# Scores from stacked rounded parts that pass through DRAM, one key block in round 0, and the sample attention in another order

## The chip, the cores and the metric

One core of one Trainium2 chip. The metric is the device time of one execution in microseconds (us), as the median of a few runs.

## The reference

One layer of a decoder for a prompt of 1024 tokens and 8 samples of 4 tokens (1056 tokens, `TOK`), all in float32, with 16 query heads of 64 on 4 key heads, a window of 128, and a mixture of 32 experts behind it. What matters here is the attention:

```python
q, k, v, xl, yl, ga, gr = split(h @ w_in)          # h = norm(x) * (1 + scale) + shift
q, k = rope(q), rope(k)
s = einsum('...qhgd,...khd->...hgqk', q, k) * 64 ** -0.5
s = where(0 <= q_pos - k_pos <= 128 and k_pos >= 0, s, -1e30)
m = maximum(max(s), sink);  p = exp(s - m)
o = (p / (sum(p) + exp(sink - m))) @ v
```

For the prompt it is banded: a block of 128 queries sees its own 128 keys and the 128 before. The first block has nothing before it. A sample sees 128 cached keys and its 4 new ones. A recurrent branch (convolution, gates, scan, GeLU) runs on `xl` and `yl`; both branches, the output projection and the experts follow.

## The kernel before

Every engine has a list of instructions written out by hand, and they meet in semaphores. A float32 product is either an f32 matmul or three products of rounded parts: `up` is the value rounded to the engine's fp32r format, `low` what is missing, and up x up + up x low + low x up comes close to the exact product (`three`, `project`). Values lie with features on the partitions; the 1056 tokens are three groups of 352 columns (`GC`), here called thirds.

1. **Projections of k, v and q** (60 to 197 us). Per chunk of 128 features, `project` makes three thirds of 24 products; ScalarE takes them out of PSUM (`keep`), copies them with halves exchanged (`swap`), and VectorE rotates (`rope`) into `kT` and `oT`. `m` counts the chunks from 2 to 9 for the queries. In between TensorE computes pieces of the adaLN vector from `w_ada` (`ada_piece`, tiles `wlate`, two buffers; SP loads piece n once piece n - 2 is used). SP's queue also holds the next weights (`wA`, `wB`) and the stores of the rounded activations (`h_store`).
2. **Sample attention** (198 to 233 us): `first_out(0)` (the first third of the next projection), pieces 14 and 15, the scores of all 8 samples in one go, `first_out(1)`, softmax on VectorE and ScalarE, transposes, 64 small products with the cached values, `first_out(2)`.
3. **Eight rounds** (233 to 580 us), one for each block of 128 queries. A round has 8 units; a unit has two heads of 64 features on the two halves of the partitions. GpSimd copies each half of `oT` into `qst`, whose other half is zero (L961), and one f32 matmul a head with all 128 partitions of `kT` gives 128 x 256 scores (previous and own block; round 0 has a zero block before). VectorE masks and takes the maximum (`first`, L1613), ScalarE exponentiates (L1186), VectorE scales (`second`, L1623 and L1624), TensorE transposes a unit later (L2320), VectorE or ScalarE copies (L1704, L1212), TensorE multiplies with the values, ScalarE puts the outputs in place of the queries in `oT` (L1215), from where SP stores them. Between a round's units stand 12 projection and gate products of the recurrent branch (`outs`, spread by `halves_at`), and VectorE and ScalarE do the convolution, gates and scan of the chunk before (`conv`, `lru_step`). Round 0 has the other adaLN products instead (`slab`, 16 loads of 0.5 MB by `slab_half` into a ring of four).

In `pe_round` a unit's place is this, s counting from 0 to 9:

```python
scores(s);  slab(s) if begin else outs(i, s);  transposes(s - 1);  values(s - 2)
```

so the transposes of unit 4 stand behind the scores and projection products of unit 5. The order of the engines' lists around it is fixed. Behind the rounds follow the projections of both branches, the router and the experts, which the change leaves alone.

Of the kernel before, what the change touches and what calls it, by code (L numbers as in the profile page):

```python
# [17 lines left out]
P = 128  # L18
D = 1024
# [159 lines left out]
def build(nc, I, O):  # L179
    ctx = ExitStack()  # L180
    with ctx:
# [11 lines left out]
        oT = at("oT", [P, KC, TOK], big)  # L193
# [61 lines left out]
        masks = at("masks", [P, BLKS, 2 * P], wv0, BF16)  # L255
# [21 lines left out]
        pS = at("pS", [P, NB, P + NT], tmp0 + 512)  # L277
        pZ = at("pZ", [P, NB * 36], tmp0 + 512 + 1056)
        pTs = at("pTs", [P, NB, P], tmp0 + 512 + 1056 + 288)
        pTn = at("pTn", [NS, NB, P], tmp0 + 512 + 1056 + 288 + 1024)  # L280
        ss0 = tmp0 + 512 + 1056 + 288 + 2048
# [6 lines left out]
        qst = at("qst", [P, 4, 2, P], u0)  # L288
        pp = at("pp", [P, 2, 2, 2 * P + 1], u0 + 1024)
        pT = at("pT", [P, 2, 4, P], u0 + 1024 + 1024 + 32)  # L290
# [153 lines left out]
        hp_dram = [nc.dram_tensor(n, [P, KC, TOK], F32) for n in ("hp_up_dram", "hp_low_dram")]  # L444
        o_dram = nc.dram_tensor("o_dram", [P, KC, TOK], F32)
# [8 lines left out]
        ld_c, ld_first, ld_small, ld_late = sem("ld_c"), sem("ld_first"), sem("ld_small"), sem("ld_late")  # L454
        ld_wada = [sem(f"ld_wada{i}") for i in range(PIECES)]
        ld_rows = [sem(f"ld_rows{i}") for i in range(LF)]
        ld_rope, ld_kc, ld_wV = sem("ld_rope"), sem("ld_kc"), sem("ld_wV")
# [3 lines left out]
        ld_spread, ld_samples, ld_route, ld_xin, ld_masks = sem("ld_spread"), sem("ld_samples"), sem("ld_route"), sem("ld_xin"), sem("ld_masks")  # L461
# [12 lines left out]
        pads_set = sem("pads_set")  # L474

# [6 lines left out]
        u_staged, u_scores, u_negmax, u_exp = sem("u_staged"), sem("u_scores"), sem("u_negmax"), sem("u_exp")  # L482
# [33 lines left out]
        st_side, st_kws = sem("st_side"), sem("st_kws")  # L516
# [14 lines left out]
        def lane_part(ap, lane):  # L531

            return ap[NS * lane:NS * (lane + 1), 0:FD].rearrange("r (h c) -> r h c", h=2)

# [67 lines left out]
        def _(sp):  # L602

            sp.dma_start(cT[:, :, :], I["cT"]).then_inc(ld_c, 16)
# [35 lines left out]
            sp.dma_start(cosT[:, :], I["cos"]).then_inc(ld_rope, 16)  # L640
            sp.dma_start(sinT[:, :], I["sin"]).then_inc(ld_rope, 16)
# [4 lines left out]
            for n in range(4, 10):  # L646
                ada_piece(n)
                if n in (5, 6):
                    sp.dma_start(kcx[:, n - 5, :, 0:P], I["kcT"][:, n - 5]).then_inc(ld_kc, 16)
                if n == 7:  # L650
                    sp.dma_start(vc[:, :, :], I["v_cache"].rearrange("b k n -> k b n")).then_inc(ld_kc, 16)
            for m in range(2, 10):
# [7 lines left out]
                if m == 9:  # L660
                    for n in (14, 15):
                        ada_piece(n)
                h_store(m - 2)
# [18 lines left out]
            def o_store(i):  # L682

                sp.wait_ge(u_out, 4 + KC * (i + 1))
                sp.wait_ge(st_o, 16 * (i + 1))
                sp.dma_start(o_dram[:, :, i * P:(i + 1) * P], oT[:, :, i * P:(i + 1) * P]).then_inc(st_o, 16)
# [35 lines left out]

            slab_half(16)
            slab_half(17)
            sp.wait_ge(s_pe, 1)
            sp.wait_ge(st_kws, 32)
            slab_half(18)
            sp.wait_ge(s_pe, 6)
            slab_half(19)
            sp.wait_ge(s_dve, 9)  # L730
            sp.dma_start(o_dram[:, :, SEQ:TOK], oT[:, :, SEQ:TOK]).then_inc(st_o, 16)
# [4 lines left out]
            for i in range(1, KC):  # L736
                lg_weights(i)
                o_store(i - 1)
# [5 lines left out]
            sp.wait_ge(u_out, 4 + KC * BLKS)  # L744
# [183 lines left out]
            sp.wait_ge(st_side, 16 * 4)  # L928
            sp.wait_ge(st_kws, 32)

        @block.gpsimd
        def _(pool):
# [7 lines left out]

            pool.wait_ge(h_split, KC)
            pool.wait_ge(hs_stage, 3 * PIECES)
            pool.memset(kT[:, :, 0:P], 0.0).then_inc(pads_set, 1)
            pool.memset(vtok[:, 0, :], 0.0).then_inc(pads_set, 1)

            pool.wait_ge(rope_done, 10)
            pool.wait_ge(v_kept, TILES)
            pool.wait_ge(s_dve, 9)
            pool.wait_ge(st_kws, 32)
            pool.wait_ge(ld_small, 16 * N_SMALL)  # L950
            pool.wait_ge(ld_late, 16 * N_LATE)
            pool.wait_ge(ld_masks, 16)
            pool.memset(qst[:, :, :, :], 0.0).then_inc(u_staged, 1)
            pool.wait_ge(u_staged, 1)
            pool.sem_inc(u_out, 4)
            for i in range(BLKS):
                for u in range(KC):
                    pool.wait_ge(u_out, 8 * i + u + 1)
# [60 lines left out]
        def _(act):  # L1019
# [7 lines left out]
            act.wait_ge(ld_c, 16)  # L1027
# [43 lines left out]
            act.wait_ge(pads_set, 2)  # L1071
# [23 lines left out]
            for t in range(TILES):  # L1095
# [3 lines left out]
                if t == 4:  # L1099
                    round_pair(0, 2)  # L1100
            act.wait_ge(v_kept, TILES)

            act.dma_start(masks[:, :, :], I["masks"]).then_inc(ld_masks, 16)
# [4 lines left out]
            act.dma_start(O["kwp"], kT[:, :, SEQ:SEQ + P]).then_inc(st_side, 16)  # L1108
            for m in range(2, 10):
# [1679 lines left out]
```

## Time and profile before

| | |
|---|---|
| median of 3 runs | 1685.8 us (1685.08 to 1690.02) |
| the profiled execution | 1685.88 us, its span 1684.0 us |
| TensorE (PE), its weight loads (PEld) | 95%, 69% of the span |
| VectorE (DVE), ScalarE (ACT), GpSimd (POOL) | 44%, 37%, 8% |
| mean granted TensorE clock | 0.983 of full speed |
| DMA | 404.66 MB, mean 240 GB/s |
| copy with rounding, 128 x 1024, ScalarE | 1.06 us |
| difference of rounded parts, 128 x 1024, VectorE | 1.23 us |
| maximum with mask of 256 columns, and scaling of 256, spacing on VectorE | 0.40 us, 0.27 us |
| copy of 512 columns out of PSUM, VectorE | 0.60 us |

How to read it: TensorE's share is that of a span in which its instructions overlap, so a high share says that it seldom waits, not that it is at its peak. The granted clock is 1.00 at 2.4 GHz and 0.50 at 1.2 GHz; a value between is a mean over a stretch with both. PE MATMUL rows of f32 products count two instructions for one matmul.

### The profile page before, as it was taken

The page shows a single profiled execution, that of the slowest core. Times are in us where ns is not written, and L with a number is a line of the kernel's source. Part 1 is how long each engine was busy: PE and PEld are TensorE (multiplying, and loading weights), DVE is VectorE, ACT ScalarE, POOL GpSimd, SP SyncE. Part 2 cuts the span into 40 slices and gives each one's busy share as a digit, 9 for nine tenths or more (in the row PEclk, how much of TensorE's full clock was granted, in tenths as well). Part 3 has the DMA queues.
Part 4 walks back from the last instruction along what each step waited for, and adds up shares of the span by engine and source line. Part 5 has one row for each costly group of instructions (what it writes and reads, how often), then busy time and mean ns, then how long its engine had stood idle before and what let it go on. Part 6 is the DMA issues. An engine that isn't in the chain of part 4 may idle for free. (4 is left out here: it accounts for less than half of the span.)

```text
span 1684.0 us, 27184 instructions
## 1 busy us (share of the span) xinstructions
PE 1601.7 (95%) x11089; PEld 1161.9 (69%) x11089; DVE 743.4 (44%) x1468; ACT 625.8 (37%) x1130; POOL 126.9 (8%) x218
## 2 busy tenths in 40 slices
PE   6999989999999989999999999988998999999997
PEld 2889877888888889999999989762333333333344
DVE  3523446888888773454555457670000000000006
ACT  4526435666666653343444354411110111111113
POOL 0000011111111000000000030000000000000012
PEclk9999999999999999999999999988999999999998
DMA  9464561111111286373457564879999999999988
GB/s 359 169 212 154 163 209 60 54 46 51 54 54 55 73 290 202 125 275 126 135 174 234 188 203 147 338 280 391 424 398 428 425 425 423 406 408 399 408 326 318
DMA packets 98866, 404.66 MB, mean 240 GB/s; under 512 B 13431, under 2 KB 42135, under 8 KB 85800
## 3 DMA queue, kind: packets, MB, share of 16 engines
q1 hardware_dynamic: 86736, 380.23, 59.6%
q0 software_dynamic: 6992, 17.78, 2.7%
q10 hardware_dynamic: 5016, 4.93, 1.0%
q8 instruction: 88, 1.44, 0.4%
q14 instruction: 34, 0.28, 0.1%
HBM read 364.83 MB, written 44.32 MB: 243 GB/s over the span
## 5 line engine op out<-in xcount | busy, mean ns | idle before, releaser
L1236 ACT ACTIVATE wup<-wraw 128x1024 fp32r<-128x1024 f32 x120 | 126.7, 1059 | 266.0 <-PE ps L2109 221.5
L1730 DVE TENSOR_TENSOR wlow<-wraw,wup 128x1024 fp32r<-128x1024 f32 x112 | 136.9, 1224 | 148.9 <-ACT wup L1236 148.3
L2109 PE MATMUL ps<-wg,xT 128*32 128x512 f32 (+2 forms) x1072 | 156.8, 612 | 11.4 <-DMA wg<-w_gate 10.6
L2109 PE MATMUL ps<-wd,aT 128*32 128x512 f32 (+2 forms) x1072 | 148.5, 593 | 6.8 <-DMA wd<-w_down 5.4
L2109 PE MATMUL ps<-wu,xT 128*32 128x512 f32 (+2 forms) x1072 | 150.3, 597 | 3.3 <-DMA wu<-w_up 3.3
L2109 PE MATMUL ps<-h_up,wup 128*128 128x384 f32 (+1 forms) x384 | 125.7, 327 | 3.5 <-DVE wlow L1730 3.5
L2109 PE MATMUL ps<-h_up,wlow 128*128 128x384 f32 (+1 forms) x384 | 124.5, 324 | 0.0
L2109 PE MATMUL ps<-h_low,wup 128*128 128x384 f32 (+1 forms) x384 | 124.5, 324 | 0.0
L2109 PEld LDWEIGHTS ps<-wd,aT 128*32 128x32 f32 (+2 forms) x1072 | 46.8, 117 | 105.1 <-issue 103.3
L2109 PEld LDWEIGHTS ps<-wg,xT 128*32 128x32 f32 (+2 forms) x1072 | 44.9, 119 | 105.7 <-issue 102.5
L1186 ACT ACTIVATE pp<-pp,ngm 128x257 f32<-128x257 f32 x128 | 64.3, 504 | 122.8 <-DVE ngm L1613 122.2
L2109 PEld LDWEIGHTS ps<-wu,xT 128*32 128x32 f32 (+2 forms) x1072 | 46.4, 117 | 91.8 <-issue 89.8
L2109 PE MATMUL ps<-hp_up,wA_up 128*128 128x352 f32 x312 | 108.5, 348 | 1.1 <-DVE hp_low L1490 1.1
L2109 PE MATMUL ps<-hp_up,wB_up 128*128 128x352 f32 x312 | 106.1, 340 | 1.6 <-ACT gB L1162 1.6
L2109 PE MATMUL ps<-hp_low,wA_up 128*128 128x352 f32 x312 | 102.0, 327 | 0.0
L2109 PE MATMUL ps<-hp_up,wA_low 128*128 128x352 f32 x312 | 101.9, 327 | 0.0
L2109 PE MATMUL ps<-hp_up,wB_low 128*128 128x352 f32 x312 | 100.7, 323 | 0.0
L2109 PE MATMUL ps<-hp_low,wB_up 128*128 128x352 f32 x312 | 100.6, 323 | 0.0
L1426 ACT ACTIVATE aT<-ps 128x512 f32<-128x512 f32 x20 | 11.9, 597 | 230.1 <-PE ps L2602 230.1
L2051 DVE TENSOR_TENSOR sgm<-sgm,ps 128x512 f32<-128x512 f32 x20 | 13.8, 688 | 167.7 <-ACT sgm L1418 167.7
L961 POOL COPY qst<-oT 64x128 f32<-64x128 f32 x128 | 57.1, 446 | 278.9 <-ACT oT L1215 274.5
L2109 PEld LDWEIGHTS ps<-h_up,wup 128*128 128x128 f32 x384 | 73.1, 190 | 4.7 <-issue 4.4
(416 smaller groups left out, 3243.6 us busy)
## 6 DMA issues: line engine op xcount, KB each, us to landing
wg<-w_gate SPq DMA_DIRECT2D x32, 2048.0 KB, 14.8
wu<-w_up SPq DMA_DIRECT2D x32, 2048.0 KB, 15.4
wd<-w_down SPq DMA_DIRECT2D x32, 2048.0 KB, 14.1
wraw<-w_ga SPq DMA_DIRECT2D x24, 512.0 KB, 3.5
wraw<-w_gr SPq DMA_DIRECT2D x24, 512.0 KB, 3.9
wraw<-w_at SPq DMA_DIRECT2D x24, 512.0 KB, 3.5
wraw<-w_lr SPq DMA_DIRECT2D x24, 512.0 KB, 3.5
wraw<-w_out SPq DMA_DIRECT2D x24, 512.0 KB, 3.7
```

What stands on the lines that cost most here:

```text
L961: pool.tensor_copy(qst[half, u % 4, a, :], oT[half, u, i * P:(i + 1) * P]).then_inc(u_staged, 1)
L1186: ins = act.activation(pp[:, s % 2, a, :], pp[:, s % 2, a, :], ACT.Exp, bias=ngm[:, s % 2, a:a + 1], scale=-1.0, accum_out=sme[:, s % 2, a ...
L1236: act.activation(wup[n % UP][:, :, :], wraw[n % RAW][:, :, :], ACT.Copy).then_inc(w_rounded, 1)
L1426: act.activation(aT[:, :, :], ps[:, 6, :].rearrange("p (m c) -> p m c", c=P), ACT.Copy).then_inc(a_kept, 1)
L1730: V.tensor_tensor(low_part(n)[:, :, :], wraw[n % RAW][:, :, :], wup[n % UP][:, :, :].bitcast(F32), ALU.subtract).then_inc(w_split, 1)
L2051: V.tensor_tensor(sgm[:, :], sgm[:, :], ps[:, 2, :], ALU.mult).then_inc(ch_moe, 1)
L2109: return pe.matmul(out, lhsT, rhs, start=start, stop=stop, skip_group_check=True)
```

## The change

It has five parts.

- **Parts of q and k.** ScalarE rounds the 1024 prompt columns of each key chunk and each rotated query chunk, VectorE subtracts, SP stores both parts to `k_dram` and `q_dram`: eight stores of 64 partitions x 2 x 1024 for the keys (each half head twice), four of 64 x 1024 for each query chunk.
- **Scores.** For a head, `qst` holds the upper part of its 64 features on partitions 0 to 63 and the lower part on 64 to 127; `kst` holds the keys' upper part twice over each other, and their lower part likewise. Two rounded products, accumulated, take the place of one f32 product. SP loads keys by block (two buffers) and queries by half block (three); GpSimd's copies and its two memsets go.
- **Round 0** works on the own block alone: 128 columns in scores, mask, exp, scaling, transposes, copies, values. One mask remains.
- **Sample attention** in the order below, softmax by bank and by half.
- **Outputs** go to `oS` and `oSs`, which wait for the store of the round before.

```diff
+            sp.wait_ge(kq_split, 2)
+            for part in range(2):
+                for a in range(2):
+                    for half in range(2):
+                        sp.dma_start(head_rows(k_dram, half).rearrange("d (p a) x n -> d p a x n", p=2)[:, :, a, part, :],
+                                     head_rows(k_part(part), a)).then_inc(st_kq, 16)
+            def q_store(u):
+                sp.wait_ge(kq_split, u + 3)
+                sp.wait_ge(st_kq, kq_stored(u))
+                for part in range(2):
+                    for a in range(2):
+                        sp.dma_start(head_rows(q_dram, part)[:, u, a, :], head_rows(q_part(u, part), a)).then_inc(st_kq, 16)
...
+            def load_keys(i):
+                if i < BLKS:
+                    ge(sp, u_scores, KC * (i - 1))
+                    c0 = P if i == 0 else 0
+                    sp.dma_start(kst[i % 2][:, :, :, c0:2 * P].bitcast(F32),
+                                 k_dram[:, :, :, (i - 1) * P + c0:(i + 1) * P]).then_inc(ld_kq[i % 2], 16)
+            def load_queries(n):
+                if n < 2 * BLKS:
+                    i, u0 = n // 2, 4 * (n % 2)
+                    ge(sp, u_scores, 4 * (n - 3) + 4)
...
+                    sp.dma_start(qst[n % 3][:, :, :, :].bitcast(F32), q_dram[:, u0:u0 + 4, :, i * P:(i + 1) * P]).then_inc(ld_kq[i % 2], 16)
...
+            sp.wait_ge(st_kq, kq_stored(KC))
+            sp.wait_ge(s_dve, 6)
+            load_keys(0)
+            load_queries(0)
+            load_queries(1)
...
+            load_keys(1)
+            load_queries(2)
...
+                load_queries(2 * i + 1)
+                load_keys(i + 1)
+                load_queries(2 * i + 2)
                 o_store(i - 1)
...
-                    for a in range(2):
-                        half = slice(HD * a, HD * a + HD)
-                        pool.tensor_copy(qst[half, u % 4, a, :], oT[half, u, i * P:(i + 1) * P]).then_inc(u_staged, 1)
...
+                        if s == 2:
+                            act.wait_ge(st_o, 16 * (i + 1))
+                            act.wait_ge(st_kq, kq_stored(KC))
+                        act.activation(oS[:, s - 2, :], ps[:, 7, 0:P], ACT.Copy).then_inc(u_out, 1)
...
-            first_out(0)
-            ada_piece(14)
-            ada_piece(15)
+            for o in range(2):
+                first_out(o).then_inc(proj_done, 1)
...
-            first_out(1)
-            pe.wait_ge(s_dve, 8)
+            ada_piece(14)
+            ada_piece(15)
+            first_out(2, range(0, 2))
...
-                            out = ps[:, 3 + s % 2, a * 2 * P:(a + 1) * 2 * P]
-                            ins = mm(out, qst[:, s % 4, a, :], kT[:, s // 4, bass.ds(i * P, 2 * P)], True, True)
+                            out = ps[:, 3 + s % 2, a * 2 * P + c0:(a + 1) * 2 * P]
+                            for part in range(2):
+                                ins = mm(out, qst[n % 3][:, s % 4, a, :], kst[i % 2][:, 2 * (s // 4) + a, part, c0:], part == 0, part == 1)
```

How the change moves instructions, at two places. First TensorE, the sample attention before: from the end of `first_out(0)` (the last `hp_up,wA_low` above) the pieces of w_ada (`wlate`), mask and scores of the samples (`mask_s`, `kcx`), and later, behind 24 products of `first_out(1)`, the transposes (`ident`) and the values (`vtok`, `vc`).

```order
L2109 MATMUL ps<-wlate_96,cE 32x512 x2
L2109 MATMUL ps<-wlate_97,cE 32x512 x2
L2109 MATMUL ps<-mask_s,identb 128x132
L2109 MATMUL ps<-kcx,qs 32x132 x4
...
L2265 MATMUL ps<-ident,pS 128x128 x4
L2269 MATMUL ps<-ident,pZ 32x128 x4
L2265 MATMUL ps<-ident,pS 128x128 x4
L2269 MATMUL ps<-ident,pZ 32x128 x4
L2109 MATMUL ps<-pTn,vtok 64x128 x4
L2109 MATMUL ps<-pTs,vc 64x16 x32
L2109 MATMUL ps<-hp_up,wA_up_98 128x352
```

The same engine now, from the sample scores, which follow `first_out(1)`, to the end of the values; of the projection products one of each piece of `first_out(2)` stands.

```order
L2194 MATMUL ps<-mask_s,identb 128x132
L2194 MATMUL ps<-kcx,qs 32x132 x4
L2194 MATMUL ps<-wlate_104,cE 32x512 x2
L2194 MATMUL ps<-wlate_105,cE 32x512 x2
...
L2353 MATMUL ps<-ident,pS 128x128 x4
L2357 MATMUL ps<-ident,pZ 32x128 x4
L2353 MATMUL ps<-ident,pS 128x128 x4
L2357 MATMUL ps<-ident,pZ 32x128 x4
L2194 MATMUL ps<-hp_up,wA_up_106 128x352
...
L2194 MATMUL ps<-pTn,vtok 64x128 x4
L2194 MATMUL ps<-pTs,vc 64x16 x32
L2194 MATMUL ps<-hp_up,wA_up_106 128x352
```

The pieces have moved behind the scores, and the last third is cut into three: 6 products ahead of the transposes, 6 behind them, 12 behind the values. Second, SP's queue at the end of the key projections, before: pieces 8 and 9 of w_ada, then 10 and 11, then the weights of the next chunk and the first store of activations.

```order
L625 DMA wlate_96<-w_ada 128x1024
L625 DMA wlate_97<-w_ada 128x1024
L625 DMA wlate_96<-w_ada 128x1024
L625 DMA wlate_97<-w_ada 128x1024
L659 DMA wA<-w_qk 128x1024
L634 DMA hp_up_dram<-hp_up 128x1056
```

And now:

```order
L646 DMA wlate_104<-w_ada 128x1024
L646 DMA wlate_105<-w_ada 128x1024
L677 DMA k_dram<-oT 128x1x1024 x8
L646 DMA wlate_104<-w_ada 128x1024
L646 DMA wlate_105<-w_ada 128x1024
L695 DMA wA<-w_qk 128x1024
L655 DMA hp_up_dram<-hp_up 128x1056
```

Eight stores of the keys' parts stand between piece 9 and piece 10.

## Rows read from the trace of the kernel before

**Rows 1.** The page: busy time, share of the span and instructions of each engine.

```profile
PE 1601.7 (95%) x11089; PEld 1161.9 (69%) x11089; DVE 743.4 (44%) x1468; ACT 625.8 (37%) x1130; POOL 126.9 (8%) x218
```

**Rows 2.** Busy time by stage: stretch, its length, engines' busy us, clock, DMA share, GB/s.

```profile
100.00:195.00 95.00, 95.00 (x578) 89.70 (x578) 35.70 (x29) 49.41 (x59) 0.00 (x0) 1.00 0.50 166
220.00:232.00 12.00, 11.20 (x103) 10.63 (x102) 0.55 (x3) 2.02 (x4) 3.25 (x9) 0.72 0.65 184
410.00:455.00 45.00, 44.55 (x292) 39.17 (x291) 37.01 (x97) 28.33 (x69) 7.73 (x16) 1.00 0.16 51
```

**Rows 3.** TensorE in order of time, round 4, then value projection: start, us, engine, instruction.

```profile
404.35 1.03 PE L2109 MATMUL ps<-kT,qst 128*128 128x256 f32 x4
...
405.38 0.32 PE L2109 MATMUL ps<-hp_low,wA_up 128*128 128x352 f32 x1
...
76.58 0.28 PE L2109 MATMUL ps<-wV_up,hp_up 128*128 128x256 f32 x1
76.70 0.29 PE L2109 MATMUL ps<-wV_low,hp_up 128*128 128x256 f32 x1
```

**Rows 4.** VectorE, ScalarE and TensorE in order of time, round 4.

```profile
406.01 0.26 DVE L1611 COPY pp<-nsink 128x2 f32<-128x2 f32 x1
419.32 0.17 DVE L1611 COPY pp<-nsink 128x2 f32<-128x2 f32 x1 [1.21 <-PE ps L2109]
423.25 2.28 DVE L1665 TENSOR_TENSOR_SCAN olst<-gC,xc 128x1024 f32<-128x1024 f32 x1
428.96 0.35 DVE L1624 TENSOR_SCALAR pp<-pp,rcp 128x256 f32<-128x256 f32 x1
...
419.41 1.28 ACT L1186 ACT_TABLE_LOAD   x1
...
429.37 0.66 PE L2320 MATMUL ps<-ident,pp 128*128 128x128 f32 x4
441.30 0.60 PE L2320 MATMUL ps<-ident,pp 128*128 128x128 f32 x4
```

**Rows 5.** Waits from 275 to 575 us: who for whom, us in total, times, longest.

```profile
PEld ps L2320 <- DVE pp L1624: 3.4, 7, 0.8
```

**Rows 6.** End of round 0: TensorE and VectorE in order of time, then stretches.

```profile
263.44 1.11 PE L2320 MATMUL ps<-ident,pp 128*128 128x128 f32 x4 [3.30 <-DVE pp L1624]
...
271.67 1.03 PE L2109 MATMUL ps<-kT,qst 128*128 128x256 f32 x4
...
248.50 0.16 DVE L1611 COPY pp<-nsink 128x2 f32<-128x2 f32 x1
263.03 0.35 DVE L1624 TENSOR_SCALAR pp<-pp,rcp 128x256 f32<-128x256 f32 x1
...
265.00:275.00 10.00, 10.00 (x45) 6.90 (x42) 1.49 (x8) 5.16 (x13) 1.14 (x4) 0.80 0.19 59
```

**Rows 7.** TensorE in order of time, sample attention.

```profile
205.67 1.05 PE L2109 MATMUL ps<-wlate,cE 128*32 128x512 f32 x4 [3.26 <-DMA wlate<-w_ada]
...
219.42 0.66 PE L2265 MATMUL ps<-ident,pS 128*128 128x128 f32 x4 [3.20 <-DVE pZ L1589]
...
222.19 0.65 PE L2109 MATMUL ps<-pTn,vtok 32*64 32x128 f32 x8 [0.80 <-ACT pTn L1131]
222.78 4.37 PE L2109 MATMUL ps<-pTs,vc 128*64 128x16 f32 x64
...
232.99 1.02 PE L2109 MATMUL ps<-kT,qst 128*128 128x256 f32 x4
```

**Rows 8.** DMA issues: transfer, queue, count, KB each, median us to landing.

```profile
wslab<-w_ada SPq DMA_DIRECT2D x16, 512.0 KB, 4.8
```

**Rows 9.** SP's issues, TensorE's use of piece 10, and one us of stores.

```profile
104.06 0.33 SPq L625 DMA_DIRECT2D wlate<-w_ada  x1
...
118.05 1.05 PE L2109 MATMUL ps<-wlate,cE 128*32 128x512 f32 x4
...
144.00:145.00 1.00, 1.00 (x9) 1.00 (x8) 0.29 (x1) 0.97 (x2) 0.00 (x0) 1.00 1.01 414
```

More of the change, by code:

```diff
@@ L192, in build @@
         hT = at("hT", [P, KC, TOK], 0)
[L193 removed]
+        oT, q_low = at("oT", [P, KC, TOK], big), at("q_low", [P, KC, TOK], big, F32R)
+        kst = [at(f"kst{i}", [P, 4, 2, 2 * P], w, F32R) for i, w in enumerate((big, big + 5 * D))]
+        qst = [at(f"qst{i}", [P, 4, 2, P], big + (2 + i) * D, F32R) for i in range(3)]
+        oS, oSs = at("oS", [P, KC, P], big + 7 * D), at("oSs", [P, KC, NS], big + 8 * D)
         hp_low, hp_up = at("hp_low", [P, KC, TOK], 0, F32R), at("hp_up", [P, KC, TOK], 2 * big, F32R)
@@ L533, in lane_part, with k_part, q_part, kq_stored @@
             return ap[NS * lane:NS * (lane + 1), 0:FD].rearrange("r (h c) -> r h c", h=2)
+        def k_part(part):
+            return oT[:, 2 + 2 * part:4 + 2 * part, 0:SEQ]
+        def q_part(u, part):
+            return q_low[:, u, 0:SEQ].bitcast(F32) if part else oT[:, (u + 3) % KC, 0:SEQ]
+        def kq_stored(units):
+            return 16 * 8 + 64 * units
+        def head_rows(ap, a):
+            return ap[HD * a:HD * a + HD]
         def bc(ap, shape):
@@ L1181, in act_round @@
             def act_round(i, first=False):
+                c0 = P if first else 0
                 for s in range(KC + 2):
@@ L1563, in _, with split_query @@
                     split_pair(0, 2)
+            for p in range(2):
+                dve.wait_ge(kq_rounded, p + 1)
+                V.tensor_tensor(k_part(1)[:, p].bitcast(F32R), kT[:, p, P:P + SEQ], k_part(0)[:, p], ALU.subtract).then_inc(kq_split, 1)
+            def split_query(u):
+                dve.wait_ge(kq_rounded, u + 3)
+                V.tensor_tensor(q_low[:, u, 0:SEQ], oT[:, u, 0:SEQ], q_part(u, 0), ALU.subtract).then_inc(kq_split, 1)
             for m in range(2, 10):
                 split_pair((m + 1) % 2, (m + 1) // 2 + 1)
+                if m > 2:
+                    split_query(m - 3)
                 rope(m, oT[:, m - 2, :])
@@ L2270, in _ @@
                 ins.then_inc(s_pe, 1)
+            first_out(2, range(2, 4))
             pe.wait_ge(s_act, 5)
@@ L2317, in pe_round @@
                         for a in range(2):
-                            for hf in range(2):
+                            for hf in blocks:
                                 q = 2 * a + hf
@@ L2730, in constants @@
     out = np.float32(-1e30)
-    masks = np.zeros((P, BLKS, 2 * P), np.float32)
-    masks[:, :, :P] = np.where(k >= q, 0, out)[:, None, :]
-    masks[:, :, P:] = np.where(k <= q, 0, out)[:, None, :]
-    masks[:, 0, :P] = out
+    masks = np.zeros((P, 2 * P), np.float32)
+    masks[:, :P] = np.where(k >= q, 0, out)
+    masks[:, P:] = np.where(k <= q, 0, out)
     t, j = (m % NT)[:, None], np.arange(P + NT)[None, :]
```

226 lines of the change are left out of this document (126 added, 100 removed).

## The prediction

> **What bounds the kernel now.** I read the page first, then the busy time by stage, then the order in time of single stretches, then the waits. TensorE is busy for 95% of the span [rows 1], so the question in every stage is whether it is the engine that the stage ends on. In the projection stage (100 to 195 us) it never pauses and the DMA engines are half used; in the 12 us before the attention rounds its clock is at 0.72 on average; a later round keeps it 44.5 of 45 us busy, but VectorE is busy for 37.0 of 45 beside it [rows 2]. The orders in time show its waits, in the sample attention and in round 0. So there are three places to cost, and everything behind 580 us moves with them.
>
> **Later rounds (1 to 7).** One unit's two f32 score products take 0.87 us: first at 404.35, and the second projection product starts at 405.38, of which 0.16 is its own spacing [rows 3]. The new form is four rounded products with the same 256 columns. Rounded products with 256 columns start 0.12 us apart in the value projection [rows 3], so 0.48: 0.39 saved a unit, 3.1 a round, if TensorE sets the pace. It doesn't quite. In round 4 VectorE takes up unit 0 at 406.01 and from there its work is a chain: it pauses once for TensorE (1.21 us before 419.32), but the exp of unit 3 cannot start before 420.7 anyway, because ScalarE has a table load (419.41, 1.28 us) ahead of it, behind the square root. Then come the scan (2.28 us) and unit 4, whose scaling is at 428.96, and TensorE's transposes of unit 4 start at 429.37, when that is done [rows 4]. TensorE waits there already: 7 times from 275 to 575 us, 3.4 us in all on the weight side [rows 5]. From 406.01 to 429.3 are 23.3 us that lose nothing. From 429.37 to 441.30 (11.9 us) TensorE sets the pace and saves two score units, 0.78. From there the chain is evacuation, square, gate products, tanh, two VectorE passes, until VectorE takes the next unit 0; it holds no scores, so it stays. The third part is what is left of the period, (404.35 - 271.67) / 3 = 44.2 us [rows 3, 6]: 9.0. I take 0.78 + 0.06 for the wait gone = 0.84 a round, 5.9 in seven. Bounds: 0.3 a round (only the present wait goes) to 3.1. GpSimd's 16 copies a round (L961) go, and nobody waits for them: nothing. Late next is VectorE. In their place SP issues 2 MB of loads a round; the DMA engines are 0.16 busy there [rows 2], and the loads are for a later half round or the next round, so they hide. They stand ahead of the store of the outputs, whose landing ScalarE now awaits before unit 0 of the next round is written. It writes that just before the table load at 419.4, 15 us after the round's first scores [rows 3, 4]; 2.6 MB at 319 GB/s (51 / 0.16) take 8 us, and with 2 or 3 for issue and landing some 4 are left. If that cover goes, each us is paid in each round, since ScalarE's table load is behind it.
>
> **Sample attention.** Now TensorE waits 3.26 us for piece 14 of w_ada until 205.67, has the sample scores behind pieces 14 and 15, waits 3.20 for the softmax before 219.42 and 0.80 before 222.19, runs much of the 64 small products (4.37 us) and of the last projection third at half clock, and begins round 0 at 232.99 [rows 2, 7]. In the new order the second projection third (24 products 0.16 apart, 3.85 us) is ahead of the scores and the two pieces behind them. Step by step, with the durations of now: thirds 0 and 1 until 206.0; scores 4.2 (as now, from 207.9 to 212.1), until 210.1; VectorE's three maxima go along by bank and end at 211.2; the last exps and the sum until 212.5; half the scaling 213.7, the other half 215.3 (an addition of 0.69 is between them); transposes until 216.3, copies 217.0; 0.6 for eight products and 64 x 0.05 (half of which ran so before the clock fell) until 221; the last half of third 2, 1.92, until 222.9. The last query part must be rounded (1.06), split (1.23), stored and, with block 0 of the keys, loaded again before the first scores; SP awaits all stores for that. Its 1 MB follows about 4.7 MB that are queued from 197.4 on. With the store rate below it is back at 223.5. **9.5 us earlier** (bounds 8 and 10).
>
> **Round 0.** It lasts 38.7 us (232.99 to 271.67), with VectorE the bound at its end: TensorE waits 3.30 us for it before 263.44, and then has a clock of 0.80 [rows 6]. One key block halves the softmax work. By the rows, max 0.40 to about 0.27 and scaling 0.27 to about 0.15, twice a unit, the copy 0.60 to 0.35 for every other: VectorE's units 4 to 7 last 12.3 us instead of 14.9 (248.50 to 263.4). But the adaLN slabs don't get shorter. They pass a ring of four, 4.8 us to landing [rows 8]; with the products on them a unit takes 2.75 us at best, and ahead of slabs 20 and 21 there now are 1.5 MB more (keys of block 1, queries). I place slab 2 at 10.5 us into the round (now 6.5), unit 4 at 14.5, and 12.3 + 6.5 for the chain and the gates: 33.3. **5.4 us less** (bounds 3.5 and 9). The 128-column rounded products have no row; four of them cost between 0.24 (half of 0.48) and 0.87, and neither end decides, since slabs and VectorE do.
>
> **What is added before.** Ten roundings on ScalarE (1.06) and ten subtractions on VectorE (1.23) lie in stages where these are 49 and 36 of 95 us busy: nothing. The stores are another matter. Eight stores of 0.52 MB, 4.2 MB in all, go into SP's queue behind piece 9 (issued at 104.06) and ahead of piece 10, which TensorE uses at 118.05 [rows 9]. Each takes 64 partitions; no row shows such a store. Bounds: the rate of full-width stores, 414 GB/s [rows 9], 10 us; or the same bytes per partition and second, 207, 20 us. The nearest row is the full-width store in the same queue, but the second reading breaks no row either, and opposite halves follow each other and may overlap: I take the middle, 15 us. From 107 (piece 9 is through) to 122, piece 10 at 124.5: a wait of 6.5 (bounds 1.5 and 12). Such a gap may drop the clock: now 3.2 us of waiting are followed by about 7 us at half speed, which cost 0.28 of 12 us, 3.4 [rows 2, 7]; I take 1.5 (bounds 0 and 3.4). **8 us more** (1.5 to 15). Later iterations (three thirds, 11.5 us) hold 2.6 MB, and hide at either rate.
>
> The Trainium skill (SBUF — State Buffer, "Door 1: The DMA port swizzle") says that 64 partitions reach 8 of 16 ports, and that a 1 MiB transfer on them moves 196 GB/s against 328 on all; under "Can I just issue two DMAs to hit both halves?" it says they serialize. It speaks against my middle value; by it, called an estimate, the stores last 21 us and piece 10 is 13 us late. No row here shows it.
>
> **Sum**: +8 - 9.5 - 5.4 - 5.9 = -12.8 us. The profiled execution is at 1685.88 us (its span 1684.0), the median of the runs at 1685.8, so both give 1673.
>
> **Rivals.**
> 1. *Half-rate stores.* For it: the layout, half the partitions in each store. Against: alternate halves can overlap. Wait and clock +15, round 0 only 8 earlier and 3.5 shorter, rounds -5.9: -2.4, so 1683. This is the case in which the rule quoted above holds.
> 2. *Full-rate stores.* +1.5, -10, -7, -5.9: 1664.
> 3. *TensorE keeps the pace in the rounds.* If VectorE's chain gives way (GpSimd leaves it more of the memory, or the exp moves up), 3.1 x 7 = 22 instead of 5.9: 1657. Against it: the wait at every unit 4.
> 4. *Slower than before.* One mechanism, the key stores ahead of piece 10 in SP's queue. From about 180 GB/s downwards (23 us) they eat all gains; at 150 they last 28 us, piece 10 waits 20, with 3.4 for the clock; round 0 then is 5 earlier and 3 shorter: 23.4 - 5 - 3 - 5.9 = +9.5, so 1695. For it: the output copies of ScalarE's queue run at the same time. Against: stores of 4 KB runs reach 414 now.
> 5. *It doesn't do what it says*: rounded products with two operands of their own as dear as the f32 ones. Then the rounds give 0.3 or less, the rest stays: 1678. The value projection's rows speak against it; it lies inside the forecast's range.
>
> **How the numbers follow.** A measurement of this kernel tells some 0.3%, 5 us, from no change: 1680.7 to 1690.9 is "the same". Forecast with rival 5: 0.35 (its own range 1665 to 1681); rival 1: 0.27; rival 2: 0.13; rival 3: 0.12; rival 4: 0.13. Faster: 0.34 + 0.13 + 0.12 and 0.08 of rival 1 = 0.67; same: 0.01 + 0.19 = 0.20; slower 0.13. The range from 1657 to 1690 leaves out half of rival 3 and most of rival 4.
>
> **What would show it.** TensorE's wait for wlate near 118 us: 6.5 us right, under 2 rival 2, over 11 rival 1, 20 rival 4. Sample scores right behind the second third, and no half clock before round 0. First scores near 223.5 plus the wait's delay. In round 0 waits for wslab rather than for VectorE. Rounds 43.2 us apart, with about 2 us of TensorE idle before the unit 4 transposes; 41 us apart would be rival 3, over 44 a wait for the output store. I'd be wrong if the wait for stored parts before round 0 is over 5 us, or if a later stage changes its length.

## The result, and the profile after

The median went from 1688.5 us (9 runs) to 1696.3 us (9 runs): ratio 1.0046, 95% interval 1.0025 to 1.0067, so slower by 0.5%. The forecast was 1673, the range 1657 to 1690. The profiled execution of the changed kernel has a span of 1691.7 us against 1684.0.

The page of the changed kernel (busy us of each engine, share of the span, instructions):

```profile
PE 1578.2 (93%) x11041; PEld 1145.4 (68%) x11041; DVE 748.9 (44%) x1484; ACT 635.4 (38%) x1140; POOL 68.5 (4%) x87
```

Stretches of it: start and end, length, busy us of each engine, granted clock, share of the DMA engines, GB/s.

```profile
100.00:195.00 95.00, 84.79 (x501) 78.60 (x500) 37.93 (x31) 48.33 (x57) 0.00 (x0) 0.95 0.71 241
107.00:124.00 17.00, 9.31 (x54) 7.79 (x52) 3.77 (x3) 5.27 (x6) 0.00 (x0) 0.90 0.96 283
237.58:280.31 42.73, 30.76 (x605) 23.07 (x605) 21.44 (x84) 17.01 (x63) 0.00 (x0) 0.73 0.69 238
322.02:365.22 43.20, 40.50 (x287) 35.94 (x285) 35.58 (x97) 27.41 (x68) 0.00 (x0) 1.00 0.33 101
365.22:409.93 44.71, 42.00 (x286) 37.12 (x285) 35.67 (x97) 27.76 (x68) 0.00 (x0) 0.96 0.32 99
409.93:456.04 46.11, 43.40 (x287) 38.53 (x285) 35.68 (x97) 27.77 (x68) 0.00 (x0) 0.93 0.31 95
```

TensorE does 23.5 us less work, and the span is 7.7 us longer: it now waits. Between 100 and 195 us it is busy for 84.8 us where it never paused [rows 2], round 0 (237.58 to 280.31) has a clock of 0.73 with the DMA engines 0.69 busy, and rounds 2, 3 and 4 (the last three) do the same work in 43.2, 44.7 and 46.1 us. The waits of TensorE (who for whom, us in total, times, longest):

```profile
PE ps L2414 <- DVE pp L1707: 15.8, 8, 2.4
...
PE ps L2194 <- DMA wslab<-w_ada: 11.2, 6, 6.5
PE ps L2194 <- DMA wlate<-w_ada: 11.1, 2, 10.2
...
PE ps L2194 <- DMA qst<-q_dram: 5.0, 1, 5.0
```

Before the change VectorE's `pp` stood there with 4.0 us, `wlate` with 3.9 and `wslab` with 0.8, and `qst` had no wait. In these four the two traces differ most. Cut at the same instructions in both traces, the stages are (us):

| stage | before | after | difference | forecast |
|---|---|---|---|---|
| start to piece 6 of w_ada | 95.2 | 93.4 | -1.8 | 0 |
| piece 6 to piece 12 (projections) | 102.1 | 114.4 | +12.3 | +8 |
| piece 12 to the first scores | 35.7 | 29.8 | -5.9 | -9.5 |
| round 0 | 38.7 | 42.7 | +4.1 | -5.4 |
| rounds 1 to 7, until the wait for `gB` | 310.8 | 312.0 | +1.2 | -5.9 |
| from there to the end | 1101.6 | 1099.4 | -2.2 | 0 |
| sum | 1684.0 | 1691.7 | +7.7 | -12.8 |

The first and the last row are not the change's: over the profiles of all kernels here but g, the last stage lies between 1096.7 and 1101.6 and the start between 93.2 and 98.1, in no order that follows the edits. Round 0 spreads as well: up to its end the changed kernel, b and c (below) have the same code, and it lasts 42.7, 44.2 and 47.4 us in their traces, at clocks of 0.73, 0.69 and 0.62. So +4.1 is the low end of what these traces show there. Behind the other four stand these rows, in order of time (start, us, engine, line, instruction, count, [idle before <- what ended it]): TensorE at piece 10, SP's key stores, TensorE ahead of round 0 and at slab 2, and SP in the same stretch.

```profile
126.51 1.92 PE L2194 MATMUL ps<-wlate,cE 128*32 128x512 f32 x4 [10.21 <-DMA wlate<-w_ada]
...
102.61 15.38 SPq L677 DMA_DIRECT2D k_dram<-oT  x8
...
237.58 1.08 PE L2194 MATMUL ps<-kst,qst 128*128 128x128 f32 x4 [5.02 <-DMA qst<-q_dram]
...
253.76 2.27 PE L2194 MATMUL ps<-wslab,cE 128*32 128x64 f32 x64 [6.51 <-DMA wslab<-w_ada]
...
220.53 3.68 SPq L686 DMA_DIRECT2D q_dram<-oT  x2
...
226.04 1.57 SPq L651 DMA_DIRECT2D wslab<-w_ada  x2
...
230.19 0.60 SPq L731 DMA_DIRECT2D kst<-k_dram  x1
230.83 7.00 SPq L741 DMA_DIRECT2D qst<-q_dram  x2
237.94 0.99 SPq L651 DMA_DIRECT2D wslab<-w_ada  x2
...
239.59 0.86 SPq L731 DMA_DIRECT2D kst<-k_dram  x1
240.50 4.16 SPq L741 DMA_DIRECT2D qst<-q_dram  x1
...
245.35 14.48 SPq L651 DMA_DIRECT2D wslab<-w_ada  x8
```

TensorE waited 10.2 us for piece 10, which SP could issue only after 15.4 us of key stores. Ahead of round 0 it waited 5.0 us for the stored queries. In round 0, slab 2 came 16.2 us after the first scores (253.76 - 237.58), where it came at 6.5 before: SP spent 7.0 us on the two loads of queries, since the second waits for the landing of the first, and had the halves of slab 1 and everything behind it still to issue. TensorE in order of time, round 4 (before it, the unit 4 transposes of round 2):

```profile
347.20 0.65 PE L2414 MATMUL ps<-ident,pp 128*128 128x128 f32 x4 [2.39 <-DVE pp L1707]
...
430.06 0.74 PE L2194 MATMUL ps<-kst,qst 128*128 128x256 f32 x4
...
435.12 1.12 PE L2414 MATMUL ps<-ident,pp 128*128 128x128 f32 x4 [2.40 <-DVE pp L1707]
...
437.22 1.23 PE L2194 MATMUL ps<-kst,qst 128*128 128x256 f32 x4
```

One of the units behind the first three in round 4 before the change, and that round as a stretch:

```profile
436.49 1.13 PE L2109 MATMUL ps<-kT,qst 128*128 128x256 f32 x4
...
404.35:448.43 44.08, 43.63 (x285) 38.25 (x284) 36.09 (x97) 27.50 (x67) 7.72 (x17) 1.00 0.16 52
```

The four score products take 0.58 us of TensorE at full clock (0.74 less the 0.16 by which the next product overlaps), where two f32 ones took 0.97 (1.13 less 0.16). That is 0.39 a unit, as forecast, and TensorE's busy time in a round falls by 3.1 us, from 43.63 to 40.50 (round 2 above). But the wait for unit 4 is 2.40 us long now, and behind it the transposes last 1.12 instead of 0.65 and the four score products 1.23 instead of 0.74: the clock is at its half level, 1.2 GHz. In round 2 the wait is as long (347.20) and the clock stayed full.

### The profile page after: what moved, and what is told of

The parts are those of the page before. It is cut to its first block and busy times, and to the rows that moved or that the text cites. A ratio compares the mean times of both kernels' runs of the same rounds, so it can differ in the third digit from the quotient of the medians.

```text
span 1691.7 us, 27036 instructions
## 1 busy us (share of the span) xinstructions
PE 1578.2 (93%) x11041; PEld 1145.4 (68%) x11041; DVE 748.9 (44%) x1484; ACT 635.4 (38%) x1140; POOL 68.5 (4%) x87
## 5 line engine op out<-in xcount | busy, mean ns | idle before, releaser
L2194 PEld LDWEIGHTS ps<-wd,aT 128*32 128x32 f32 (+2 forms) x1072 | 47.0, 117 | 106.0 <-issue 104.2
L2194 PEld LDWEIGHTS ps<-wg,xT 128*32 128x32 f32 (+2 forms) x1072 | 44.7, 119 | 106.0 <-issue 102.8
L1246 ACT ACTIVATE pp<-pp,ngm 128x257 f32<-128x257 f32 (+1 forms) x128 | 62.6, 491 | 116.7 <-DVE ngm L1696 116.0
L2194 PE MATMUL ps<-hp_up,wA_up 128*128 128x352 f32 x312 | 101.7, 326 | 1.3 <-DVE hp_low L1554 1.3
L2131 DVE COPY xT<-ps 128x512 f32<-128x512 f32 x21 | 14.5, 692 | 134.1 <-PE ps L2661 134.0
## 6 DMA issues: line engine op xcount, KB each, us to landing
wu<-w_up SPq DMA_DIRECT2D x32, 2048.0 KB, 15.4
```

Of the source, the lines that this page charges most:

```text
L1246: ins = act.activation(pp[:, s % 2, a, c0:], pp[:, s % 2, a, c0:], ACT.Exp, bias=ngm[:, s % 2, a:a + 1], scale=-1.0, accum_out=sme[:, s % ...
L2131: V.tensor_copy(xT2[n % 2][:, 4:8, :], ps[:, 1, :].rearrange("p (k c) -> p k c", c=P)).then_inc(x_high_half, 1)
L2194: return pe.matmul(out, lhsT, rhs, start=start, stop=stop, skip_group_check=True)
```

## The experiments

All ratios are to the kernel before the change, measured in the same session, from 7 to 10 runs of each kernel, but only four of e, g, j, k and l; the changed kernel's is 1.0046. The stages come from one trace of each. The stages are those of the table above, in us: projections / to first scores / round 0 / rounds 1 to 7.

| kernel | ratio (interval) | projections | to scores | round 0 | rounds 1-7 |
|---|---|---|---|---|---|
| before | 1 | 102.1 | 35.7 | 38.7 | 310.8 |
| after | 1.0046 (1.0025-1.0067) | 114.4 | 29.8 | 42.7 | 312.0 |
| a_keys_behind | 1.0060 (1.0039-1.0082) | 117.6 | 31.1 | 47.7 | 313.3 |
| b_fill | 1.0011 (0.9992-1.0030) | 115.4 | 29.8 | 44.2 | 304.1 |
| c_half_moved | 0.9952 (0.9932-0.9973) | 114.6 | 30.0 | 47.4 | 294.1 |
| d_slabs_first | 1.0031 (1.0018-1.0045) | 115.3 | 32.5 | 39.3 | 313.3 |
| e_full | 0.9865 (0.9826-0.9904) | 103.5 | 30.6 | 38.7 | 294.4 |
| f_before_moved | 0.9991 (0.9971-1.0012) | 102.1 | 39.4 | 39.3 | 307.8 |
| g_full_width | not used, see there | 109.9 | 33.0 | 44.0 | 311.9 |
| h_spread | 1.0017 (0.9993-1.0040) | 103.7 | 32.0 | 43.9 | 313.4 |
| i_one_block | 0.9961 (0.9942-0.9980) | 102.1 | 35.4 | 35.7 | 310.7 |
| j_pieces_first | 0.9815 (0.9796-0.9834) | 104.1 | 27.8 | 36.9 | 294.5 |
| k_before_best | 0.9933 (0.9916-0.9950) | 102.1 | 39.1 | 35.6 | 307.8 |
| l_busy_wait | 0.9875 (0.9856-0.9894) | 106.0 | 31.2 | 39.4 | 294.5 |

**Rounds: is it the clock?** b repeats the scores of unit 5, useless work in front of the wait:

```diff
-                        for a in range(2):
+                        for a in (0, 1) if begin or s != 5 else (0, 1) * 6:
                             out = ps[:, 3 + s % 2, a * 2 * P + c0:(a + 1) * 2 * P]
```

> The changed kernel; in rounds 1 to 7 TensorE repeats the four score products of unit 5 five more times (20 useless products, about 2.4 us), just ahead of the place where it waits 2.4 us for unit 4. Theory (the clock falls behind that wait and costs 1.5 us a round in rounds 3 to 7): more work, and the rounds last 43.2 us each at a full clock, 8 us less in all: 1688. Rival (the longer rounds come from VectorE or from the loads): the rounds stay at 44.7 or grow, and the time is 1696 or more.

Round 4 of b as a stretch:

```profile
414.21:457.39 43.18, 42.87 (x306) 38.35 (x305) 35.55 (x97) 27.39 (x68) 0.00 (x0) 1.00 0.32 102
```

Rounds 2 to 6 last 43.2 us each at full clock, with 20 products more in them, and rounds 1 to 7 last 304.1 us instead of 312.0. That is 7.9 us by the trace and 0.35% (6 us) between the ratios, whose intervals overlap a little, so the trace tells it more firmly than the times. The clock theory held.

c and f put useful work there, the first half of output 4, in the changed kernel and in the one before:

```diff
-            return (((0, 0),), ((0, 1), (1, 0)), ((1, 1), (2, 0)), ((2, 1),), ((3, 0),), ((3, 1),), ((4, 0), (4, 1)), ((5, 0), (5, 1)),
+            return (((0, 0),), ((0, 1), (1, 0)), ((1, 1), (2, 0)), ((2, 1),), ((3, 0),), ((3, 1), (4, 0)), ((4, 1),), ((5, 0), (5, 1)),
```

> The changed kernel; in the rounds the first half of output 4 (12 products, 2.0 us) stands in unit 5's place, ahead of the wait for unit 4, instead of in unit 6's. Theory (TensorE has 2 us of free time there and sets the pace behind it): no wait over 0.5 us, no half clock, and rounds of about 41.5 us instead of 44.6 on average: 20 us less, 1676. Rival (VectorE's chain sets the round's end too): the rounds stay at 43.2, 9 us less, 1687. If neither the wait nor the clock matters: 1696.

> The kernel before the change, with only the half of output 4 moved ahead of the wait for unit 4. Theory (there TensorE waits only 0.5 us for unit 4, and only the 2 us of that half are moved, not saved): rounds shorter by 0.3 to 0.5 us, 3 us in all, 1686. Rival (the move alone is worth what it was worth in the changed kernel): 16 us, 1673; then the rounded scores would have no part in that gain.

TensorE in round 4 of c, in order of time:

```profile
436.53 0.66 PE L2414 MATMUL ps<-ident,pp 128*128 128x128 f32 x4 [0.45 <-DVE pp L1707]
...
448.04 0.66 PE L2414 MATMUL ps<-ident,pp 128*128 128x128 f32 x4 [1.10 <-DVE pp L1707]
```

That round as a stretch:

```profile
411.37:453.41 42.04, 40.50 (x286) 35.91 (x285) 35.36 (x97) 27.38 (x68) 0.00 (x0) 1.00 0.33 104
```

The round lasts 42.0 us at a clock of 1.00, 17.9 us less in seven. Waits of 0.45 and 1.10 us are left, and neither is followed by a slower clock. In the kernel before, the same edit takes 3.0 us off the rounds (310.8 to 307.8) and nothing measurable off the time. So the difference of c and f, 13.7 us in seven rounds or 2.0 a round, is what the rounded scores, with GpSimd's copies gone and the loads in their place, are worth once their gap is filled. TensorE's work falls by 3.1 a round, which is what rival 3 of the prediction had put; the waits that are left in c keep about a third of it.

**Projections: order, width or bandwidth?** a puts all eight key stores behind pieces 10 and 11:

```diff
-            sp.wait_ge(kq_split, 2)
-            for part in range(2):
...
             for m in range(2, 10):
                 if m < 4:
                     for n in (2 * m + 6, 2 * m + 7):
                         ada_piece(n)
+                if m == 2:
+                    sp.wait_ge(kq_split, 2)
+                    for part in range(2):
...
```

> The changed kernel with its eight key stores issued behind pieces 10 and 11 of w_ada instead of ahead of them. Theory (order in SP's queue): TensorE's wait of 10.2 us for piece 10 and the 1.9 us at half clock behind it go, the projections end 12 us earlier, and the time is about 12 us under the changed kernel's: 1684. Rival (the DMA engines are what is short, so the stores cost wherever they stand): the weights of the fourth query chunk, or piece 12, come late instead, a wait of 5 us or more shows there, and the time is 1690 or more.

TensorE's one wait between 100 and 200 us, and SP's key stores, in order of time:

```profile
143.44 0.66 PE L2195 MATMUL ps<-hp_up,wA_up 128*128 128x352 f32 x1 [12.40 <-DVE wA_low L1547]
...
117.34 15.12 SPq L691 DMA_DIRECT2D k_dram<-oT  x8
```

What the rival named came: pieces 10 and 11 are on time, and the next weights in the queue come 12.4 us late. I had not reckoned that they are needed only 5 us after piece 11, so this trace doesn't say whether the DMA engines or the order are at fault. h spreads the same stores: two behind piece 9, two behind piece 10, four behind the weights.

```diff
...
+            key_store(0, 0, 0)
+            key_store(0, 0, 1)
...
+                        if n == 10:
+                            key_store(0, 1, 0)
+                            key_store(0, 1, 1)
...
+                if m == 2:
+                    for a in range(2):
+                        for half in range(2):
+                            key_store(1, a, half)
```

> The changed kernel with its key stores apart: two behind piece 9, two behind piece 10, four behind the weights of the fourth query chunk. Theory (only the length of the row of stores ahead of a load makes TensorE wait; the engines have room when the stores are spread): no wait over 2 us and no half clock from 100 to 200 us, projections 12 us shorter, 1684. Rival (as with all eight behind piece 11, where the 12.4 us only moved to the next weights): the wait turns up at piece 10, piece 11 or the query weights, with more than 5 us in sum, 1692 or more.

The only wait left between 100 and 210 us is 1.3 us (for `wB_low`), and the stage is back at 103.7. So it was the length of the row of stores. The engines had room over the stage (0.76 busy from 100 to 195 us), but not all through it: from 111 to 145 us they are 0.96 busy in h, and nobody waits for them. The time fell by less than the stage (1.0046 to 1.0017, 5 us of 10.8, with intervals that overlap): the wait for the first queries grew to 7.3 us, and round 0 and the later rounds were 2.7 us longer.

g stores from 128 partitions, as many bytes:

```diff
-                for a in range(2):
+                for p in range(2):
                     for half in range(2):
-                        sp.dma_start(head_rows(k_dram, half).rearrange("d (p a) x n -> d p a x n", p=2)[:, :, a, part, :],
-                                     head_rows(k_part(part), a)).then_inc(st_kq, 16)
+                        sp.dma_start(k_dram[:, 2 * p + half, part, :], k_part(part)[:, p, :]).then_inc(st_kq, 16)
```

> The changed kernel with its eight key stores from 128 partitions by 1024 instead of 64 by 2048: as many bytes and stores, in the same place in SP's queue. What is stored is not in the order in which it is read, so the attention is computed on the wrong keys; times and amounts are as before. Theory (64 partitions are what makes the stores slow): the eight last 11 to 14 us instead of some 21, TensorE's wait for piece 10 falls from 10.2 to under 4 us, and the time is about 8 us less, 1688. Rival (writes to DRAM in rows of 4 KB, or other transfers beside them, set the rate): the wait stays over 8 us, 1696.

TensorE at piece 10 and SP's key stores in g, in order of time:

```profile
122.89 1.92 PE L2193 MATMUL ps<-wlate,cE 128*32 128x512 f32 x4 [5.00 <-DMA wlate<-w_ada]
...
104.21 5.25 SPq L677 DMA_DIRECT2D k_dram<-oT  x8
```

The stretch of g in which they move:

```profile
107.00:121.00 14.00, 10.90 (x62) 8.49 (x60) 3.78 (x3) 5.72 (x7) 0.00 (x0) 1.00 0.95 377
```

The wait is 5.0 us instead of 10.2, and with the DMA engines equally busy (0.95 and 0.96) the rate is 377 GB/s against the 283 of the changed kernel's 107 to 124 us above; SP is through the eight issues in 5.3 us instead of 15.4. So half the partitions account for 5.2 us of the wait, and the same bytes ahead of a piece that is due still cost 5.0 us at full width. Of the whole stage the width is worth 4.5 of 12.3 us (109.9 us against 114.4). The result lies between theory (under 4) and rival (over 8), nearer to the theory. Of g only this stage counts: with wrong attention the router chooses otherwise, and from `gB` to the end it takes 1120.4 us.

**Round 0 and the wait ahead of it.** d reorders SP's queue in round 0:

```diff
             load_queries(0)
-            load_queries(1)
...
             slab_half(19)
...
-            load_keys(1)
-            load_queries(2)
+            slab_half(20)
+            slab_half(21)
+            load_queries(1)
...
+            for n in range(24, N_LATER):
+                slab_half(n)
+                if n == 26:
+                    load_keys(1)
+                if n == 28:
+                    load_queries(2)
```

> The changed kernel; in round 0 SP issues slab halves 18 to 21 ahead of the second half's queries, and the keys and queries of round 1 behind slab halves 26 and 28. Theory (SP stands still for the first loads and issues the slabs behind 2 MB that are not needed yet): the waits for wslab fall from 11.2 to under 4 us, the clock in round 0 rises from 0.69, and round 0 lasts 34 to 36 us instead of 42.7: about 7 us less, 1689. Rival (the DMA engines are short of bandwidth there, whatever the order): the wait moves to the queries or the keys, and round 0 stays over 40 us, 1695.

Round 0 went from 42.7 to 39.3 us and the waits for `wslab` from 11.2 to 5.5: between the two expectations. The clock didn't rise (0.69, and 0.73 in the changed kernel). 39.3 is also below all five traces in which SP's queue in round 0 is as in the changed kernel (42.7 to 47.7: itself, a, b, c and h). But the wait ahead of it was 7.7 us instead of 5.0, and the ratio (1.0031) can't be told from the changed kernel's. How far round 0 spreads without d shows in c:

```profile
239.28:286.68 47.40, 34.54 (x604) 25.05 (x605) 21.53 (x84) 17.03 (x63) 0.00 (x0) 0.62 0.64 215
```

i does the one-block round alone, in the kernel before:

```diff
-                w = s % 2
+                w, c0 = s % 2, 0 if i else P
...
-                    ins = V.tensor_tensor_reduce(pp[:, w, a, 0:2 * P], ps[:, 3 + w, a * 2 * P:(a + 1) * 2 * P],
+                    ins = V.tensor_tensor_reduce(pp[:, w, a, c0:2 * P], ps[:, 3 + w, a * 2 * P + c0:(a + 1) * 2 * P],
...
```

> The kernel before the change, with only the first round on one key block (128 columns in scores, softmax, transposes and values); no stored parts, no other order. The prediction's step (VectorE's units get 0.65 us shorter each, slabs as before): VectorE's wait at the end of round 0 shrinks, round 0 lasts 35 to 36 us instead of 38.7: 3 us less, 1683. Rival (the slab loads or the gates' chain at the end set its length): 38 us or more, no difference.

35.7 us, as expected: one block is worth 3.0 us as long as the slabs come as before (35.6 in k below, against 39.3 in f). e takes four edits together (c, h, d, and: three pairs of `h_store` put off to round 1, the last query stores ahead of the sample outputs):

> The changed kernel with four edits together: the half of output 4 moved ahead of the wait for unit 4; the key stores two by two behind pieces 9 and 10, the last four behind the weights of the fourth query chunk; slabs ahead of loads in round 0; three of the eight pairs of stores of the scaled input put off to round 1 and the last query stores ahead of the sample outputs. If the four places are where the time went: 12 from the projections, 18 from the rounds, 5 from the wait ahead of round 0 and 4 in it, 39 off the changed kernel's 1696: 1657. If the bandwidth of the DMA engines is the bound between 100 and 270 us, the first, third and fourth edits give a third of that or less: 1672.

1665.7 us, between the two: projections and rounds gave what was expected (10.9 and 17.5), but TensorE still waited 5.9 us for the first queries, and round 0 stayed at 38.7. Two reasons were open, the clock (0.50 at the start of round 0) and the DMA engines, and l and j take one each. l keeps TensorE busy through the wait:

```diff
             pe.wait_ge(s_dve, 12)
+            for n in range(56):
+                mm(ps[:, 3, 0:2 * P], wA_up[0][:, n % KC, :], hp_up[:, n % KC, 0:2 * P], True, True)
```

> The kernel with the four edits, and 56 useless products of 256 columns (some 6.5 us) on TensorE while it waits for the first stored queries. Theory (the half clock in round 0 is the consequence of that wait and costs there): the first 7 us of round 0 run at full clock, round 0 lasts 3 us less than 38.7, 1663 by a before of 1686.5. Rival (round 0 waits for slabs from DRAM, and the clock only fills time that would be idle): the waits for wslab grow by what the clock gives, and round 0 stays within 1 us of 38.7.

TensorE of l in order of time:

```profile
223.73 6.76 PE L2213 MATMUL ps<-hp_up,wA_up 128*128 128x256 f32 x56
...
254.61 1.08 PE L2213 MATMUL ps<-wslab,cE 128*32 128x64 f32 x32 [3.57 <-DMA wslab<-w_ada]
```

The beginning of round 0 as a stretch, in l:

```profile
230.33:240.00 9.67, 5.91 (x212) 4.93 (x212) 4.29 (x26) 4.30 (x20) 0.00 (x0) 0.98 0.85 261
```

The same of e:

```profile
231.74:241.50 9.76, 9.38 (x216) 8.14 (x216) 4.56 (x26) 4.68 (x21) 0.00 (x0) 0.66 0.79 248
```

The clock rose from 0.66 to 0.98, TensorE's busy time fell from 9.4 to 5.9 us, and round 0 took 39.4 us: the waits for `wslab` took it back (7.0 us against 4.6). With the four edits the clock is not what costs there. In the changed kernel itself this wasn't tried; of the three traces with its round 0, the one with the lowest clock is the longest (c), so it stays open whether the clock has a part in the 4.1 us. j puts pieces 14 and 15 back ahead of the sample scores, and the last query stores behind slabs 16 and 17, so that the slabs are issued earlier:

```diff
             for o in range(2):
                 first_out(o).then_inc(proj_done, 1)
+            ada_piece(14)
+            ada_piece(15)
...
-            ada_piece(14)
-            ada_piece(15)
             first_out(2, range(0, 2))
...
-            q_store(KC - 1)
...
             slab_half(16)
             slab_half(17)
+            q_store(KC - 1)
```

> The kernel with the four edits, and pieces 14 and 15 of w_ada again ahead of the sample scores (2 us of TensorE), so that SP can issue slabs 16 and 17 some 6 us earlier, ahead of the last query stores. Theory (behind the reordering the slab loads start 11 us later than before the change, and that is what makes the wait ahead of round 0 and those in it): the wait for the first queries falls from 5.9 to under 3 us, round 0 gets 2 us shorter, about 4 us less than the four edits: 1662 by a before of 1686.5. Rival (the last query parts' way through DRAM sets the start of round 0 whatever the slabs do): the same wait, and 2 us more: 1667.

SP and TensorE of j in order of time:

```profile
207.24 2.71 SPq L651 DMA_DIRECT2D wslab<-w_ada  x2
...
218.39 0.59 SPq L741 DMA_DIRECT2D kst<-k_dram  x1
...
225.07 0.64 PE L2213 MATMUL ps<-kst,qst 128*128 128x128 f32 x4 [0.24 <-DMA qst<-q_dram]
```

The first slabs were issued 10.0 us behind the use of piece 12 instead of 18.2 as in the changed kernel (207.24 - 197.26 and 226.04 - 207.81), the wait for the queries fell to 0.24 us, the first scores came 2.8 us and the end of round 0 another 1.8 us sooner than in e. SP did not issue the loads of keys and queries sooner (21.1 us behind piece 12, in e 20.5), but the queries were used 6.0 us after their issue instead of 9.4: in e two slab loads stand right ahead of them, in j the small query stores. The theory held, for the two moves together; which of them does how much isn't shown. j is the fastest kernel here: 1657.3 us, 1.9% under the kernel before. k asks whether the way through DRAM pays:

> The kernel before the change with one key block in round 0 and the half of output 4 moved: what there is to gain with f32 scores and no stored parts. If the two add up: 3 and 3 us less, 1681. Against the four edits' 0.9865 it says whether the rounded scores pay for their way through DRAM: by theory they do, by 12 us or more; by the rival (most of the gain of the four edits was the table and the one block) this one is at 1672 or less.

0.9933 against 0.9815 for j: without stored parts and rounded scores one block and the moved half give 0.7%, and j, which also has the new order in the sample attention, 1.9%. By the stages the rounds account for 13.3 us of the difference and the stretch to the first scores for 11.3, of which some 4 are the spread told below; the projections and round 0 give 2.0 and 1.3 of it back. So the rounded scores pay for their way through DRAM once the stores and loads stand where nobody waits long for them.

## Why the prediction was wrong, step by step

- **Key stores (+8; measured +12.3).** The mechanism and its place were right; its size lay between the forecast (a wait of 6.5 us) and rival 1 (over 11, and 15 with the clock). The failed step is the term of 15 us for the eight stores. I had taken the middle of two rates because "opposite halves follow each other and may overlap". That didn't make up for the width: SP's eight stores alternate between the halves, and all transfers together moved 283 GB/s, against 377 at full width. The rule of the Trainium skill (SBUF — State Buffer, "Door 1: The DMA port swizzle" and "Can I just issue two DMAs to hit both halves?") had put piece 10, as an estimate, 13 us late. It was used 10.3 us later, counted from piece 6: the trace agrees with the rule in its direction, and in size it lies between the rule's and mine. Width isn't all of it, since at full width (g) the wait was 5.0 us, where my bound had 1.5.
- **Sample attention (-9.5; measured -5.9).** TensorE's own part went as worked out: scores right behind the second third, transposes after a wait of 1.3 instead of 3.2 us, no half clock up to 231 us. The failed sentence is "With the store rate below it is back at 223.5": the queries came 5.0 us late, not in time. I had counted the bytes ahead of the last query part, but not the 1 MB of slabs 16 and 17 that SP issues between it and the loads (226.04, and the loads at 230.19); at the 267 GB/s of the stretch from 230.2 to 237.6 us they take an estimated 3.9 us, and the scores came 3.6 behind their place (29.8 us behind piece 12, forecast 26.2). With the slabs ahead of the query stores, for which pieces 14 and 15 have to be used earlier, the wait is gone (j, 0.24 us).
- **Round 0 (-5.4; measured +4.1).** The step that failed is "I place slab 2 at 10.5 us into the round": it came at 16.2. The saving by one block is 3.0 us (i), as long as the slabs are on time. What was missed is that `load_queries(1)` makes SP stand until the first queries have landed, with slab 1 behind it (d: 3.4 us), and the late slabs (j: 1.8 us, by one trace each). The forecast named waits for `wslab` instead of VectorE in round 0, and that is what the trace shows, at 11.2 us instead of about 4. The rest of the loss isn't divided: the same code spreads over 4.7 us with its clock.
- **Rounds 1 to 7 (-5.9; measured +1.2).** Round 2 lasts 43.20 us with a wait of 2.39 us before unit 4, and the forecast said 43.2 and about 2; the 0.39 saved a unit was right too. But I let that wait cost nothing. In rounds 3, 5, 6 and 7 the clock falls behind it and takes some 1.5 us, in round 4 2.9. I had priced exactly this for the projections ("such a gap may drop the clock") and had the row for it, and did not apply it to the gap that my own forecast made. With the clock kept up (b) the rounds are 6.7 us shorter than before the change, and 5.9 was the forecast. The sign "over 44 a wait for the output store" came without such a wait: the half clock brought it alone.
- **Output store, GpSimd, roundings (0).** Right: no wait for the output store, and the longer rounds have ScalarE and VectorE as busy as the short ones.
- **The mark for being wrong** was a wait for stored parts of over 5 us; it came at 5.02, just over the mark. Rival 4 had the sign and the time (1695) but not the cause: it had the wait at 20 us, and it was 10. No rival held two or three middling losses together, and that is how it went: three of the four terms came out beyond the bad end of their bounds. Two of them, the sample attention and round 0, did so where stores, queries and slabs stand in one queue, and I had summed them as if they were apart; the third is the clock in the rounds.

## What to carry to other kernels

When an engine gets faster inside a round that another engine paces, its saved time becomes a gap; ask at once whether the clock falls in it, and move later work into it, or the saving turns into a loss. A transfer that is put into a busy queue can cost most of its length at the first load behind it that is due (10.2 and 12.4 us here, for stores that SP issues in 15): place it by due times, a few at a time, use all partitions, and look for waits of the queue's own engine that hold up what stands behind. Terms that draw on the same queue are not to be summed with independent bounds.

## What the runs showed that I had not expected

- A wait of 2.4 us was followed by the full clock in round 2 and by the half clock in rounds 3 to 7 of the same kernel; waits of 0.91 (round 1) and of 0.45 and 1.10 us (c) never were. What decides between the two cases of 2.4 us stays open.
- Twenty useless products in the gap cost nothing and gave back 7.9 us. In round 0 of e, where transfers decide, the same trick gave nothing.
- The stretch from piece 12 to the first scores varies by 4 us in kernels that have the old order unchanged (35.4, 35.7, 39.1 and 39.4), with the same waits and a clock of 0.91 (before, 197 to 233 us) or 0.79 (k, 195 to 235 us). The -5.9 us of the table are counted from one of the short ones.
- Why e's projections last 103.5 us and l's 106.0 with the same code isn't settled. A single profile tells the projections to some 2 us, the stretch to the first scores to 4, and round 0 of the changed kernel to 5.
